# Factor of the input norm applied to the projections' outputs instead of the input tiles, and two small columns loaded as rows

## The reference, cut to what matters

```python
def rmsnorm(x, w):
    y = x * lax.rsqrt(jnp.mean(jnp.square(x), axis=-1, keepdims=True) + EPS)
    return y * w
...
h = jnp.concatenate([meta_tokens, x], axis=1)              # (1, 1040, 1024)
proj = rmsnorm(h, norm_mix_pre) @ w_in
c_q, c_kv, k_rope, z, xbc, dt_raw = jnp.split(proj, IN_OFFSETS, axis=-1)   # 384, 256, 64, 1024, 1536, 16
...
xbc = jax.nn.silu(causal_depthwise_conv(xbc, conv_w, conv_b))              # 4 taps along the positions
xs, bm, cm = jnp.split(xbc, (1024, 1024 + 256), axis=-1)
...
y = y + d_skip[head] * xs
ssm = gated_group_rmsnorm(y, z, ssm_norm)                                  # y * silu(z), norm, weight
```

## Time and profile before

| | us |
|---|---|
| median of three timed runs | 1630.07 (1629.95 to 1630.63) |
| profiled execution, its time | 1633.88 |
| its span, first to last instruction | 1632.1 |
| TensorE busy | 1578.7 (97%) |
| VectorE, ScalarE, GpSimd busy | 934.3, 606.1, 819.9 |
| mean granted clock of TensorE, share of full | 0.991 |

### The profile page before, as it was taken

The page is one execution under the profiler, slowest core; times in us unless marked ns, Lnnn a source line. Parts: engine busy times, 40 slices in busy tenths (PEclk is TensorE's granted clock), DMA queues, the critical chain, the costliest instruction groups (busy, mean ns, idle before and its releaser), DMA issues.

```text
span 1632.1 us, 23489 instructions
## 1 busy us (share of the span) xinstructions
PE 1578.7 (97%) x8143; PEld 1356.3 (83%) x8143; DVE 934.3 (57%) x1547; ACT 606.1 (37%) x1177; POOL 819.9 (50%) x775
## 2 busy tenths in 40 slices
PE   6899999999999999999999999999999999999995
PEld 5899998878888888788887888888888888888884
DVE  4565515156767667676778767844444444444446
ACT  6222311244444444455554342333333333333333
POOL 7252554145667657943312430755555555555553
PEclk9999999999999999999999999999999999999998
DMA  6343522226555455688878730111111111111116
GB/s 208 81 147 102 178 74 59 65 74 178 175 148 162 140 152 170 239 311 298 310 247 290 256 105 13 59 51 51 51 51 51 51 51 51 50 51 51 51 49 104
DMA packets 182184, 204.25 MB, mean 125 GB/s; under 512 B 18400, under 2 KB 145216, under 8 KB 182112
## 3 DMA queue, kind: packets, MB, share of 16 engines
q1 hardware_dynamic: 180816, 199.12, 38.1%
q0 software_dynamic: 1296, 4.19, 1.6%
HBM read 133.97 MB, written 69.30 MB: 125 GB/s over the span
## 4 chain that ended last, share of the span: by engine, by line
PE 83%; DMA 4%; POOL 4%; DVE 4%; SPq 2%; ACT 2%; issue 1%; POOLq 0%; DVEq 0%; ACTq 0%
PE ps L2758 17%; PE ps L2744 16%; PE ps L772 5%; PE ps L831 5%; PE ps L2604 5%; PE ps L2679 4%; PE ps L1720 3%; PE ps L2710 3%; PE ps L2724 3%; PE ps L803 2%; PE ps L1706 2%; POOL ring L172 2%; PE ps L1689 1%; POOL ring L170 1%; PE ps L2558 1%; PE ps L1637 1%
## 5 line engine op out<-in xcount | busy, mean ns | idle before, releaser
L3221 DVE TENSOR_TENSOR acc<-ps,acc 128x512 f32<-128x512 f32 x208 | 142.5, 690 | 114.8 <-PE ps L2758 114.8
L170 POOL TENSOR_TENSOR ring<-stage,zero 128x512 fp32r<-128x512 f32 (+2 forms) x83 | 90.7, 1092 | 196.0 <-PE ps L772 55.5
L2758 PE MATMUL ps<-wdhi,fshi 128*128 128x512 f32 x416 | 161.8, 389 | 0.0
L2758 PE MATMUL ps<-wdlo,fshi 128*128 128x512 f32 x416 | 161.8, 389 | 0.0
L2758 PE MATMUL ps<-wdhi,fslo 128*128 128x512 f32 x416 | 161.8, 389 | 0.0
L2494 POOL TENSOR_TENSOR wdlo<-wd_b,wdhi 128x512 fp32r<-128x512 f32 x56 | 70.7, 1296 | 140.3 <-ACT wdhi L2992 140.3
L3249 DVE TENSOR_TENSOR ps<-ps,fs_b 128x512 f32<-128x512 f32 x42 | 29.4, 699 | 150.6 <-PE ps L2744 150.6
L172 POOL TENSOR_TENSOR ring<-stage,ring 128x512 fp32r<-128x512 f32 (+2 forms) x83 | 112.3, 1353 | 6.5
L2604 PE MATMUL ps<-ring,s_aT 128*128 128x512 f32 x384 | 98.1, 398 | 3.4 <-ACT mixs L2833 3.4
L772 PE MATMUL ps<-hThi,ring 128*128 128x346 f32 (+1 forms) x480 | 95.7, 328 | 0.0
L2987 ACT ACTIVATE fs_b<-ps 128x512 f32<-128x512 f32 x42 | 25.1, 598 | 183.1 <-PE ps L2744 183.1
(11 more groups left out here) (485 smaller groups left out, 4589.3 us busy)
## 6 DMA issues: line engine op xcount, KB each, us to landing
wd_b<-w_mlp_down SPq DMA_DIRECT2D x28, 512.0 KB, 4.0
wA_b<-w_mlp_up SPq DMA_DIRECT2D x42, 256.0 KB, 2.8
stage<-w_in SPq DMA_DIRECT2D x40, 256.0 KB, 2.7
stage<-w_out SPq DMA_DIRECT2D x28, 256.0 KB, 4.6
xt<-x SPq DMA_DIRECT2D x8, 512.0 KB, 7.2
d_xT<-xdT SPq DMA_DIRECT2D x8, 512.0 KB, 3.3
d_x<-x_tok SPq DMA_DIRECT2D x8, 512.0 KB, 4.6
d_zT<-zs SPq DMA_DIRECT2D x16, 256.0 KB, 2.3
```

The lines of the kernel that those rows point to most:

```text
L170: pool.tensor_tensor(hi, src, k.zero[:, 0:1].broadcast_to([P, width]), ALU.add).then_inc(k.sem(fam + "_hi"), 1)
L2758: mm = pe.matmul(ps[:, 2 + n % 4, :], fs[a][:, j, P * t:P * t + P], half(wd[b][:, j, :], c), start=(j == 0 and a == 0 and b == 0), stop=(j ...
L3221: dve.tensor_tensor(part, ps[:, 2 + n % 4, :], part, ALU.add).then_inc(sem("v_added"), 1)
```

## The change

In phase_norm the tiles are no longer scaled: they are turned as loaded. The factors of all nine tiles are worked out once (in `stat5`, kept as `k.r_in`), multiplied into the identity (`diag`), cut in a high and a low part, and summed over the partitions by products with ones, which gives the factors as a row on all partitions (`k.rrow`). The turn order, the order of loads and the place of the small constants change. In phase_project VectorE multiplies the three pieces of a column by `rrow` where ScalarE copied them; the cq and ck copies become multiplies by the factor of the row; a multiply by `rrow` in PSUM stands ahead of each silu of z (`scaled_z`), put between VectorE's other work. The multiply by `dcol` moves to ScalarE, `conv_acc` has one buffer, `out_x` parts 0 and 1 of x stand behind the convolution on VectorE, and columns 2 to 4 take the turns of x at another place. d_skip and ssm_norm are loaded as rows in phase_norm and turned by TensorE. The cq copies stand ahead of VectorE's waits for the stores of B and C.

```diff
+O_DCOL = O_DT - 64
+O_RROW = 184672
+O_KRO = 171424
...
-    BANK = (4, 2, 1)
+    BANK = (4, 1, 2)
-    TURNS_AT = ((5,), (6,), (7,), (), (8, 9), (10, 11), (12, 13), (14, 15))
+    TURNS_AT = ((3,), (4,), (5, 6), (7, 8), (9, 10), (11, 12), (13, 14), (15,))
+    RR = ((2, 0, META), (5, META, 512), (4, META + 512, 512))
...
-        for t in ORDER[:FIRST]:
-            load_x(t)
+        sp.dma_start(k.ident[:, :], io["c_ident"]).then_inc(sem("id_in"), 16)
+        load_x(0)
+        load_x(1)
+        load_x(NT)
+        sp.dma_start(k.par[:, :], io["c_par"]).then_inc(sem("id_in"), 16)
+        load_x(2)
         load_w(0)
-        sp.dma_start(k.ident[:, :], io["c_ident"]).then_inc(sem("id_in"), 16)
-        sp.dma_start(k.par[:, :], io["c_par"]).then_inc(sem("id_in"), 16)
+        load_x(3)
         load_w(1)
         load_x(4)
+        load_w(2)
         load_x(5)
-        load_w(2)
+        load_w(3)
         load_x(6)
         load_x(7)
-        load_w(3)
...
+        sp.dma_start(cst[KD:2 * KD, 2, :], io["ssm_norm"][0].rearrange("(k p) -> k p", p=P)).then_inc(sem("d_in"), 16)
+        sp.dma_start(pairs[0:KD, 0:2], io["d_skip"].rearrange("o (k e) -> (o k) e", e=2)).then_inc(sem("d_in"), 16)
@@ phase_norm, on_scalar
+        square(0)
+        square(1)
+        square(NT)
         act.wait_ge(sem("mt"), 1)
         act.activation(hT[0][:, :, 0:META], mtmp[:, :, :], ACT.Copy).then_inc(sem("mt_hi"), 1)
+        square(2)
+        for n in range(3):
+            high(n)
+        square(3)
         high(3)
+        square(4)
         high(4)
+        square(5)
         high(5)
         high(6)
+        square(6)
+        high(7)
+        high(8)
+        square(7)
+        high(9)
+        high(10)
+        act.wait_ge(sem("v"), 1)
+        act.activation(s_, v[:, 0:NT + 1], ACT.Sqrt).then_inc(sem("sqrt"), 1)
+        for n in range(11, 2 * KD):
             high(n)
+        act.wait_ge(sem("diag"), 1)
+        act.activation(dd[0][:, :, :], diag[:, :, :], ACT.Copy).then_inc(sem("diag"), 1)
+        for n, (bank, c0, w) in enumerate(RR):
+            act.wait_ge(sem("rr"), n + 1)
+            if n == 0:
+                act.activation(own_cols[:, :], ps[:, bank, 2 * META:2 * META + 2 * KD], ACT.Copy).then_inc(sem("d_in"), 1)
+            act.activation(k.rrow[:, c0:c0 + w], ps[:, bank, 0:w], ACT.Copy).then_inc(sem("rr_out"), 1)
@@ phase_norm, on_vector, end of stats()
+            dve.tensor_tensor(diag[:, :, :], k.ident[:, :].unsqueeze(1).broadcast_to([P, NT + 1, P]), r9.unsqueeze(2).broadcast_to([P, NT + 1, P]),
+                              ALU.mult).then_inc(sem("diag"), 1)
...
+        for n in range(7):
             low(n)
         dve.wait_ge(sem("c_in"), 48)
         dve.tensor_copy(k.ident_b[:, :], k.ident[:, :]).then_inc(sem("consts"), 1)
         dve.tensor_copy(k.mask_b[:, :], cst[:, 1, :]).then_inc(sem("consts"), 1)
+        low(7)
         dve.tensor_copy(k.tri[:, :], cst[:, 0, :]).then_inc(sem("consts"), 1)
+        low(8)
         dve.tensor_scalar(k.ones[:, :], cst[:, 0, :], 0.0, 1.0, ALU.mult, ALU.add).then_inc(sem("consts"), 1)
+        dve.wait_ge(sem("d_in"), 32)
+        dve.tensor_copy(cst[0:KD, 2, :].rearrange("k (e p) -> k e p", e=2), pairs[0:KD, 0:2].unsqueeze(2).broadcast_to([KD, 2, SHD])).then_inc(sem("consts"), 1)
+        dve.wait_ge(sem("sq"), NT + 1)
+        rsqrt_before(dve, k, v[:, 0:NT + 1], ss_of, 1.0 / D, "v", 1)
+        low(9)
+        low(10)
+        stats()
+        for n in range(11, 2 * KD):
+            low(n)
+        dve.wait_ge(sem("diag"), 2)
+        dve.tensor_tensor(dd[1][:, :, :], diag[:, :, :], dd[0][:, :, :].bitcast(F32), ALU.subtract).then_inc(sem("diag"), 1)
@@ phase_norm, on_tensor
-            pe.wait_ge(sem("xn"), 2 * half + 2)
-            pe.wait_ge(sem("xa"), 2 * half + 2)
+            for i in range(4):
+                pe.wait_ge(sem(f"x_in{4 * half + i}"), 16)
...
+        pe.wait_ge(sem("t_lo"), 2 * KD - 2)
+        for kk in range(KD):
+            part(0, 1, kk, 1)
         pe.wait_ge(sem("t_lo"), 2 * KD)
-        for q in (1, 2):
-            for kk in range(KD):
-                mm = part(0, q, kk, q)
+        pe.wait_ge(sem("consts"), 5)
+        pe.wait_ge(sem("diag"), 3)
+        pe.transpose(ps[:, 2, 2 * META:2 * META + 2 * KD], cst[0:2 * KD, 2, :], k.ident[0:2 * KD, 0:2 * KD])
+        for bank, c0, w in RR:
+            for a in range(2):
+                if w == META:
+                    mm = pe.matmul(ps[:, bank, 0:w], k.ones[0:META, :], dd[a][0:META, NT, 0:META], start=(a == 0), stop=(a == 1))
+                else:
+                    t = (c0 - META) // P
+                    mm = pe.matmul(ps[:, bank, 0:w], k.ones[:, :], dd[a][:, t:t + 4, :].rearrange("p a b -> p (a b)"), start=(a == 0), stop=(a == 1))
+            mm.then_inc(sem("rr"), 1)
+        pe.wait_ge(sem("rr_out"), 1)
+        for kk in range(KD):
+            mm = part(0, 2, kk, 2)
         mm.then_inc(sem("x_done"), 1)
@@ phase_project, on_sync
-        for e in range(2):
-            sp.dma_start(k.dcol[SHD * e:SHD * e + SHD, :],
-                         io["d_skip"].rearrange("o (k e) -> o e k", e=2)[0, e].partition_broadcast(SHD), allow_slow_non_contiguous=True).then_inc(sem("d_in"), 16)
-        sp.dma_start(k.wcol[:, :], io["ssm_norm"][0].rearrange("(k p) -> p k", p=P), allow_slow_non_contiguous=True).then_inc(sem("w_in"), 16)
@@ phase_project, on_tensor
-                if kk == 2 and f == 2:
-                    turn_x(0, (0, 1))
-                if kk == (4 if f == 2 else 2) and 2 <= f <= NXT + 1:
+                if kk == {2: 2, 3: 1, 4: 1}.get(f):
+                    turn_x(f - 2, (0, 1))
+                if kk == {2: 4, 3: 3, 4: 3}.get(f, 2) and 2 <= f <= NXT + 1:
                     turn_x(f - 2, (2,))
...
-            if 2 <= f <= NXT:
+            if 4 <= f <= NXT:
                 turn_x(f - 1, (0, 1))
@@ phase_project, on_scalar, behind silu
+            if f < KD:
+                act.wait_ge(sem("xc_done"), f + 1)
+                if f == 0:
+                    act.wait_ge(sem("d_in"), 33)
+                if f >= 2:
+                    act.wait_ge(sem(f"xd_sent{f % 2}"), 16 * (f // 2))
+                act.activation(xdT[:, f % 2, :], xc[:, f % 2, META:POS], ACT.Copy, scale=k.dcol[:, f:f + 1]).then_inc(sem("xd_done"), 1)
@@ phase_project, on_vector
+            dve.wait_ge(sem("x_done"), f + 1)
+            for q, (c0, w) in enumerate(TC):
+                dve.tensor_tensor(pre[:, f % 2, 4 + c0:4 + c0 + w], ps[:, Q0_BANK[f] if f < 4 and q == 0 else 3 * (f % 2) + q, 0:w], rrow[:, c0:c0 + w],
+                                  ALU.mult).then_inc(sem("pre_out"), 1)
+            if f - 1 >= KD and f <= NXT:
                 out_x(f - 1, (0, 1))
...
+            else:
+                dve.wait_ge(sem("xc_done"), f)
+            a = acc[:, :]
...
+            if 1 <= f <= KD:
+                out_x(f - 1, (0, 1))
...
+        for t in range(NT):
+            dve.wait_ge(sem("cq_done"), t + 1)
+            dve.tensor_scalar(cqs[:, t, :], ps[:, t % 4, 0:QL], r_in[:, t:t + 1], None, ALU.mult).then_inc(sem("cq_out"), 1)
         for name in ("bt_sent", "btm_sent"):
             dve.wait_ge(sem(name), 32 * GROUPS)
...
+        def scaled_z(g):
+            dve.wait_ge(sem("z_done"), g + 1)
+            c0 = META + 512 * (g % 2)
+            dve.tensor_tensor(ps[:, g % 4, :], ps[:, g % 4, :], rrow[:, c0:c0 + 512], ALU.mult).then_inc(sem("z_scaled"), 1)
```

More of the change, by code:

```diff
@@ L239, in phase_norm @@
     xt, o = m.at("xt", [P, NT + 1, D], F32, o)
-    cst, o = m.at("cst", [P, 2, P], F32, o)
+    cst, o = m.at("cst", [P, 3, P], F32, o)
+    pairs, o = m.at("pairs", [P, 8], F32, o)
     mtmp, o = m.at("mtmp", [P, KD, META], F32, o)
-    junk, o = m.at("x_junk", [P, D], F32, o)
-    ss, v, r = k.st[0], k.st[1], k.st[3]
+    junk, _ = m.at("x_junk", [P, D], F32, o)
+    diag, o = m.at("diag", [P, NT + 1, P], F32, o)
+    dd, o = [], k.o_work
+    for s in ("hi", "lo"):
+        t, o = m.at("diag" + s, [P, NT + 1, P], F32R, o)
+        dd.append(t)
+    assert o <= k.o_work + 4 * D * 4
+    own_cols, _ = m.at("cols", [P, 2 * KD], F32, O_DCOL)
+    k.dcol, k.wcol = own_cols[:, 0:KD], own_cols[:, KD:2 * KD]
+    k.rrow, _ = m.at("r_row", [P, POS], F32, O_RROW)
+    ss, v = k.st[0], k.st[1]
+    r = k.r_in = k.st[5]
     hT = k.hT
@@ L304, in square @@
                 act.wait_ge(sem("sq"), c)
[L305 to L309, removed]
+            act.activation(junk[0:rows, :], xt[0:rows, t, :], ACT.Square, accum_out=ss[0:rows, t:t + 1]).then_inc(sem("sq"), 1)
         def high(n):
@@ L326, in on_scalar @@
[L326 to L334, removed]
+        act.activation(k.st[2][:, 16:17], ss[:, 16:17], ACT.Sqrt)
+        square(0)
+        square(1)
+        square(NT)
         act.wait_ge(sem("mt"), 1)
         act.activation(hT[0][:, :, 0:META], mtmp[:, :, :], ACT.Copy).then_inc(sem("mt_hi"), 1)
-        high(2)
-        square(7)
+        square(2)
@@ L380, in on_vector @@
```

(36 more changed lines are left out.)

107 lines of the change are left out of this document (44 added, 63 removed).

## The result

The changed kernel takes **1617.43 us** in the median of four runs (1616.17 to 1622.34, the longest of them the profiled one); the kernel before took 1630.03 beside it. The medians differ by 12.6 us. The ratio over all runs is 0.9932 with a 95% interval of 0.992 to 0.9945, which is 11.1 us (9.0 to 13.0). The profiled execution took 1622.34 us, its span is 1620.5, where before it was 1632.1: 11.6 us less. The forecast was 10.3 us, from 1630.07 to 1619.8, with a range of 1616.5 to 1625.5.

What follows compares the result with a forecast made beforehand. TensorE, busy 97% of the span, was taken as the bound, so time moves only where it idles, runs at half rate or its work changes. 4.5 + 5.8 + 0.4 - 0.4 = 10.3 us gave 1619.8 us, range 1616.5 to 1625.5.

Steps and rivals of the forecast that it cites:

- Part A: Start of the kernel: raw tiles turned once four are in, factors applied later; 4.5 us gained, between 2.0 and 7.0.
- The five small instructions of VectorE: VectorE's queue after low(6) at the start: two casts, tri, ones and the d_skip copy, 3.5 us in all.
- The half microsecond set aside for the diagonal's parts: End of column 0: high and low diagonal copies end at 41.5 to 42.6, TensorE comes at 42; half a microsecond off.
- Part B: x columns: d_skip loaded early as rows, so TensorE's wait and the half clock behind it go; 5.8 us gained.
- a sum over columns: Columns 1 to 4 of x: 31.9 us before against 26.2 reckoned at full clock, which gives 5.7.
- Part C: Latents and z: cq copies no longer queue behind stores, 0.4 gained; last z multiply not hidden, 0.4 lost.
- The wait of 0.9 stays: TensorE's 0.9 us wait for btoklo was expected to remain unchanged.
- The tail: Behind the projection of q: all edits lie before 345 us, so a shift there carries through to the end.
- Rival 1: Start gives little, VectorE's queue at upper bounds and clock late: A 1.5, whole 7.3, 1622.8 us; 14 in 100.
- Rival 2: Start gives all, no stall at turn 14, clock early: 7.0, whole 12.8, 1617.3 us; 12 in 100.
- Rival 3: d_skip wait only replaced, later out_x(0, 2) misses its turn: B gives 1, 1624.6 us; 7 in 100.
- Rivals 4 and 5: VectorE's chain becomes the bound: 1625 to 1635 us, 6 in 100; small form, 3 us, 1622.8 to 1624, 8 in 100.

Runs made afterwards that it cites:

- experiment 6: Changed kernel with low(11) and low(12) ahead of the diagonal: 1619.1 us; with tile 3's transfer also ahead of weight block 0: 1619.75 us; unaltered beside it: 1619.33 us.
- the two controls: The changed kernel unaltered, run again on two further chips beside the rearranged starts; 1619.33 us on the first, profiled spans 1620.0 and 1620.4.
- experiment 5: Changed kernel with the convolution's first step done two extra times in columns 3 to 11: 1627.21 us, the changed kernel on the same chip 1619.33.
- Experiment 4: Kernel before, with 22 unread products 346 wide filling TensorE's 3.5 us wait for d_skip: 1628.42 us beside 1629.88, ratio 0.9995.
- experiment 3: Kernel before, with the slow d_skip and ssm_norm column transfers issued earlier, among the norm stage's weight loads: 1625.97 us, ratio 0.9974.
- experiment 2: Changed kernel, but dcol and wcol loaded as before by slow column transfers at the start of the x stage: 1628.9 us, ratio 0.9993.

## Why the prediction was right, point by point

**Part A** was forecast at 4.5 us and measured 4.5 (52.08 to 47.55), partly by errors that cancel. The first turn came at 11.09, not 10.3, and the first product at 13.83, not 13.4: 0.4 lost (the 13.4 held 0.3 more than its own 10.3 + 2.8, or it would have been 0.7). Full rate came at 17.2, as forecast (17.3). The five small instructions of VectorE took 3.25 for the forecast 3.5 (0.48, 0.21, 0.71, 0.78, and 1.07 for the d_skip copy), the diagonal more (2.41 for 2.0).

Turn 14 waited 1.8 and not 1.5, with both of its ends off: TensorE stood there at 33.8, not 34.5, and the low part it needed ended at 35.5, not 36.0. That 36.0 doesn't follow from the terms beside it: 24.6 + 3.5 + 3.0 + 1.4 + 2.0, and 0.75 for `low(11)`, is 35.3, which against 34.5 is a wait of 0.8. The size of this wait was luck; its place and its cause, the diagonal in VectorE's queue, are shown by experiment 6, where it goes with the order. The sum has one more slip: 4.9 less half a microsecond is 4.4.

The row of factors took 1.4 (42.32 until products go on near 43.7; forecast 1.3). The half microsecond set aside for the diagonal's parts was not needed: its low part ended at 41.75, TensorE came at 42.32. And 4.5 is the figure of one execution: with the same code up to there, column 1 begins at 47.50 and 47.09 in the two controls and at 46.32 in the kernel of experiment 5, where the diagonal took 2.17 and turn 14 waited 1.2; that is 4.6, 5.0 and 5.8 us gained.

For the clash of VectorE and GpSimd the traces have these numbers: the convolution steps take 1.3 us alone and 2.1 beside a cut; the multiplies, which read PSUM, 1.37 for three in either case; the diagonal took 0.4 more than I had put, its low part nothing more, but GpSimd's cut at 40.50 beside it took 2.38 where the one at 43.96 took 1.28. With the rule (the Trainium skill, SBUF — State Buffer, Who interferes with whom: two SBUF operands clash with GpSimd, one in PSUM does not) the traces agree, though of the 1.5 us that a whole cut in front of each would have cost, the two new instructions cost VectorE 0.4.

**Part B** was forecast at 5.8 and gave 6.3 up to the turn at the end of column 4 (95.69 to 84.81 is 10.9, less the 4.5 of A). The direct reckoning in the prediction, idle time and half of the half-rate stretch, had said 6.3; I stayed beside a sum over columns that said 5.7, and the direct one was right. Experiment 4 shows the clock's share, 2.9 us, in the trace, and experiment 3 that the request's time is what matters.

**Part C** held in size: cq 0.5 gained (forecast 0.4), z and what is behind it 0.4 lost (forecast 0.4). It was read from this one pair of traces and not tried alone.

**The term that failed** is the sentence "The wait of 0.9 stays". It went, and is the largest error, 0.85 us. In the timelines of the kernel before and of the changed one, the steps of the convolution that the turn waits for:
```profile
161.90 5.72 DVE L1066 SCALAR_TENSOR_TENSOR conv_acc<-pre,par,conv_acc 128x1040 f32<-128x1040 f32 x3
...
171.49 1.07 PE L753 MATMUL ps<-ident,xc 128*128 128x128 f32 x8 [0.85 <-DVE btoklo L1039]
```
```profile
150.58 5.05 DVE L1085 SCALAR_TENSOR_TENSOR conv_acc<-pre,par,conv_acc 128x1040 f32<-128x1040 f32 x3
...
159.57 1.04 PE L772 MATMUL ps<-ident,xc 128*128 128x128 f32 x8
```
Three steps take 0.67 us less, and the chain is done in time. The kernels of experiments 4 and 3, where evacuation is as before, have 5.66 and 5.07 there and waits of 0.79 and 0.21: together with 5.72 and 0.85, each microsecond of the steps is one of the wait. So it is mostly the moment at which GpSimd's cut falls into the convolution that decides, not the new multiplies. By that line the changed kernel's 5.05 would still leave 0.2; what took this last part was not tried. A wait on such a chain can't be carried over as a constant when everything before it moves.

**The tail.** I let the gain carry through whole; 0.5 us of it is lost behind the projection of q. In the executions of the experiments this stretch takes from 1278.3 to 1282.2 us, against 1281.3 before and 1281.8 after, and its waits for transfers (`s_aT`, the q rows) differ from one to the next. It moves the total by more than the errors above.

**Sum.** 10.3 forecast; 11.6 in the profiled spans, 12.6, 10.5 and 10.3 in the timed medians of three chips. In the spans: 10.3 + 0.5 (B) + 0.9 (the wait) + 0.1 (C) - 0.5 (the tail) = 11.3; of the other 0.3, what is not rounding lies in columns 5 to 11 and has no row of its own. The forecast lies inside the 9.0 to 13.0 us of the first measurement and near both later ones; that several of its terms were off and partly cancelled is luck.

**The rivals.** Rival 1, a start that gives 1.5, is refuted by 4.5. Rival 2 named 1617.3, next to the measured 1617.4, but its mechanism is refuted: the stall at turn 14 is there and A gave 4.5, not 7.0. Rival 3, a wait only replaced, is refuted: none is left there; its neighbour, 1.1 us, exists in experiment 3 alone. Rivals 4 and 5 are refuted for this kernel, with rooms before the end-of-column turn of 0.5 in column 3, 3.5, 2.5 and 1.7 in columns 4, 5 and 7. Experiment 5 shows what they would have cost: with 1.6 to 3.1 us more of VectorE in a column, 8 us.

## What to carry to other kernels

A small transfer that the path waits for is worth its wait plus the half-rate stretch behind it, and an earlier arrival of the engines is worth nothing until that transfer is asked for earlier too: parts A and C alone left 1.3 us, not told from none, of a gain of more than ten. Ask for each wait ahead of the place where you gain time what releases it, and whether that moves along. Where two engines slow each other, shifting a stage by two or three microseconds changes the durations behind it (3.98 to 6.21 us here), so waits that rest on them must be reckoned anew, and a local gain is to be counted only at the next landmark behind them.

## What the runs showed of the hardware

- A wait of 3.5 us was followed by 5.6 us at a granted clock of 0.50; with the idle time filled by useless products there was none. But equal idle stretches did not end alike: 2.67 us before 86.41 in experiment 5 were followed by a clock of 1.00, 2.67 us before 165.26 by a stretch at 0.50 (the windows above). What tells the two apart the rows don't say.
- At the start the granted clock is written as 1.00 while products are at half rate. Between 13.83 and 17.2 us products 348 wide stand 0.29 us apart, behind 17.2 only 0.16, and both windows say 1.00 (TensorE in the changed kernel: busy, granted clock, DMA share, GB/s). There the spacing must be read.
```profile
13.80:17.20 3.40, 3.40 (x13) 1.00 1.05 390
17.20:20.00 2.80, 2.80 (x21) 1.00 0.74 250
```
- The transfer of ssm_norm, 4 KB of single numbers spread over the partitions, took 10.41 us from issue to landing (experiment 2), while one of 512 KB of x took 7.3 in the median at the start of the changed kernel.
- GpSimd's cuts and VectorE's steps with two SBUF operands stretch each other by how they fall: three steps of the convolution took 3.98 us with GpSimd still and 4.32 to 6.46 with it cutting, one cut 1.28 alone and up to 2.38 beside such an instruction.
